# Square sums of q and k as rows with a 16-column table, their scales through DRAM, and values one unit sooner

## Chip, cores and metric

The kernel runs on one core of a Trainium2 chip. The metric is the device time of one execution in microseconds (us), the median of several.

## The reference

One layer of a hybrid encoder in float32, for a sequence of 1024 tokens and a width of 2048. After an RMSNorm, one projection gives the columns of two head groups. The change concerns group A, eight attention heads of 128 dimensions:

```python
qa = _rope_partial(_rmsnorm(q_a.reshape(B, S, ATT_HEADS, ATT_HEAD_DIM), q_norm_w), cos, sin)
ka = _rope_partial(_rmsnorm(k_a.reshape(B, S, ATT_HEADS, ATT_HEAD_DIM), k_norm_w), cos, sin)
```

So each head needs, for q and for k, the sum of squares of every token over the 128 dimensions, and its root's reciprocal as a factor of that token; the first 32 dimensions are rotated. Banded softmax attention over three dilated windows follows, and a gate silu(z). Group B is a matrix-memory mLSTM of four heads, run in both directions. Both outputs go through one output projection and are added to x.

## The kernel before

**Layout and units.** Everything is held transposed: dimensions on the 128 partitions, tokens along the free axis. The program is written by hand as a sequence of units `u`, the same for every engine: each engine has a loop over `u` that does its share of the main products, and then calls the functions of the side work with `at = u - start`. Units 0 to 447 are the input projection in a Strassen-like form of 7 products for each of 64 groups; units 448 to 575 are the output projection. A unit on TensorE (`product`, L649 on, or `out_product`) is 12 main matmuls of 128x512 (w_hi and w_lo against t_hi and t_lo, L671 to L675; L699 to L701 in the output). ScalarE rounds the weight block (w_hi, L933) and VectorE makes the rest (w_lo, L1158) two units ahead; both evict products (`evict`), VectorE also makes the sums s_tmp (L1193 to L1214) in most units. At the start of a unit VectorE evicts the unit before, so a late VectorE holds TensorE up once it is about one unit behind. There are two banks of PSUM for the products.

**The attention heads.** Head h starts at unit 357 + 18 h (`A_START`) and runs to at = 23, so that at 18 to 23 of one head are at 0 to 5 of the next. By `at`:
- SyncE (`attention_loads`) fetches raw q and k at -4, the 32 rows to be rotated at 2 (eight small transfers, L501), writes the rotated rows back over the raw ones at 5 and 6 (L508), fetches z at 6 (L514) and v at 8 (L518), and stores y at 23 (L521). SyncE issues all loads and most stores of the kernel in program order, the weights among them; a wait in it holds back what follows. POOL issues the accumulating stores of the products.
- ScalarE squares raw q and k into a_q and a_k at 0. TensorE sums them at 1 (`square_sums`, L824): 16 fp32 matmuls, each with 128 tokens of the squares as the stationary operand and one column of ones as the moving one. The tokens are taken with a step of 4 (`to_class`), so the result is one column of sums for each block of 128 tokens, on 128 partitions.
- VectorE adds eps at 2 (L1554), ScalarE takes the root (L1089), VectorE the reciprocal at 3 (L1561): 128x16 each. TensorE spreads the columns over all partitions at 3 and 5 (`spread`, 8 transposes of a repeated column each, into PSUM banks 4 to 7).
- VectorE rotates at 4 and 5 (`rotate`, in a_q and a_k), and makes the normed q and k at 7 and 9 (`normed`, L1514) from raw, weight and the spread scale in PSUM; z is scaled at 8 (L1548) and v at 10 (L1551).
- Then, for eight blocks of queries i: scores at 10 + i (L864 to L868), masked minimum on VectorE and exponentials on ScalarE at 11 + i, the division (VectorE L1537, ScalarE L1069) and TensorE's probability transposes (L881 to L884) at 12 + i, and their copies to pT by ScalarE (L1076) and VectorE (L1586) at 13 + i. pT holds two blocks. `values` (L895 to L899) of blocks 2j and 2j + 1 come at 15 + 2j, ahead of the probability transposes of the same unit; VectorE multiplies them by the gate at 16 + 2j (L1569). The copy of block 2j + 2 waits for values(j), and the probability transposes of a block wait for both copies of the block before:

```python
if i % 2 == 0 and i > 0:
    act.wait_ge(a_pv, 4 * g + i // 2)
```

**The gate stage.** In unit 42 the same kind of sums is taken of x for the first norm: 8 matmuls with contiguous tokens (L724) for xrsc and 8 with the step of 4 (L726) for eps in the order of the classes. In unit 45 eight transposes spread xrsc.

Of the kernel before, what the change touches and what calls it, by code (L numbers as in the profile page):

```python
# [108 lines left out]
def build_program(nc, xT, w_all, w_gates, vecs, norm_cols, m_cols, att_mask, rope, eye, tri, fin, part, y_dram, outT):  # L109
    with ExitStack() as ctx:  # L110
# [31 lines left out]
        xq = sb("xq", [P, 2 * TB])  # L142
# [5 lines left out]
        qk_arg = sb("qk_arg", [P, 2 * TB])  # L148
        qk_rms = sb("qk_rms", [P, 2 * TB])
        qk_rs = sb("qk_rs", [P, 2 * TB])  # L150
# [45 lines left out]
        pT = view(5504, 6 * 256).rearrange("p (b q) -> p b q", b=6)  # L196
        cos4, sin4 = view(11776, 256), view(12032, 256)
# [111 lines left out]
        a_bc = sem("a_bc")  # L309
# [66 lines left out]
        def _(sp):  # L376
# [100 lines left out]
            def attention_loads(h, at):  # L477
# [18 lines left out]
                if at == 2:  # L496
                    sp.wait_ge(a_ss, h + 1)
                    for i, to in enumerate((a_q, a_k)):
                        src = fin[2 * GROUPS[g[i]][0] + 1 - i]
                        for k in range(4):  # L500
                            sp.dma_start(to[k * ROT:(k + 1) * ROT, 0:256],  # L501
                                         src[k // 2, 0:ROT, k % 2 * 256:(k % 2 + 1) * 256]).then_inc(turn_in[i], 16)
                if at in (5, 6):
                    i = at - 5
                    raw, to = ((raw_a, a_q), (raw_b, a_k))[i]
# [13 lines left out]
                if at == 23:  # L519
# [124 lines left out]
        def _(pe):  # L644
# [62 lines left out]
            def gates_and_norm(u):  # L707
# [12 lines left out]
                if u == 42:  # L720
                    pe.wait_ge(xg_sum, KT)
                    pe.wait_ge(prep, 3)
                    for b in range(TB):
                        nc.tensor.matmul(ps[:, 5, b:b + 1], sq_acc[:, b * P:(b + 1) * P], ones[:, 0:1],  # L724
                                         start=True, stop=True)
                        mm = nc.tensor.matmul(ps[:, 5, TB + b:TB + b + 1],  # L726
                                              to_class(sq_acc)[:, b // 2, b % 2 * P:(b % 2 + 1) * P], ones[:, 0:1],
                                              start=True, stop=True)
                    mm.then_inc(x_ss, 1)
                if u == 45:  # L730
                    pe.wait_ge(x_rs, 1)
                    pe.wait_ge(consts, 64)
                    for b in range(TB):
                        t = on_all_partitions(flat(6)[:, b * P:(b + 1) * P], xrsc[:, b:b + 1])
                    t.then_inc(x_bc, 1)
# [79 lines left out]
            def square_sums(h):  # L815
                pe.wait_ge(a_sq, 2 * h + 2)
                if h > 0:
# [4 lines left out]
                for i, src in enumerate((a_q, a_k)):  # L822
                    for b in range(TB):
                        mm = nc.tensor.matmul(ps[:, 4, i * TB + b:i * TB + b + 1],  # L824
                                              to_class(src)[:, b // 2, b % 2 * P:(b % 2 + 1) * P],
# [985 lines left out]
```

## Time and profile before

| | |
|---|---|
| median of 3 runs | 2150.01 us (2148.2 to 2152.46) |
| the profiled execution's own time | 2148.27 us |
| its span, from the first to the last instruction | 2146.1 us |
| TensorE, matmuls | busy 2068.2 us (96%) |
| VectorE | busy 1292.6 us (60%) |
| ScalarE | busy 846.7 us (39%) |
| mean granted clock of TensorE | 0.977 of full |

Times in the profile are in microseconds unless marked ns. PE is TensorE's matmul, PEld its weight load (which overlaps PE), DVE VectorE, ACT ScalarE, POOL GpSimd, SP SyncE; a q behind a name is the engine's queue. L12 is line 12 of the kernel before. An fp32 matmul has two records in the trace, a transpose and a main matmul (fp32r) one. Records of TensorE are pipelined, so from start to start is the time that one costs, and the duration shown is longer. PEclk is the granted clock of TensorE as a share of 2.4 GHz.

### The profile page before, as it was taken

How to read it: one execution, taken by the hardware profiler on the slowest of the kernel's cores; microseconds unless marked ns; L12 is line 12 of the kernel's file. 1: busy time of each engine (PE TensorE's matmuls, PEld its weight loads, DVE VectorE, ACT ScalarE, POOL GpSimd, SP SyncE). 2: the span in 40 equal slices, each digit the busy share in tenths (PEclk: the TensorE clock that was granted, in tenths of full speed). 3: DMA queues.
4: the chain of work that ended last, by engine and by line, in shares of the span. 5: the costliest groups of instructions: out<-in, count | busy, mean ns of one | idle time of the engine just before them, and what ended most of it. 6: DMA issues, size and time to landing. Idle time of an engine off the chain costs nothing.

```text
span 2146.1 us, 27457 instructions
## 1 busy us (share of the span) xinstructions
PE 2068.2 (96%) x9536; PEld 1699.7 (79%) x9536; DVE 1292.6 (60%) x2670; ACT 846.7 (39%) x1350; POOL 174.0 (8%) x156
## 2 busy tenths in 40 slices
PE   5999999999999999999999999999998999999999
PEld 3887887888888888888878878778786877878887
DVE  7777758677677667767686646464565434343222
ACT  5553325344344335335453344352536343342110
POOL 4340000110110110010001101000010000000000
PEclk9999999999999999999999999999999999999999
DMA  4552344652562553463436535253344514235443
GB/s 161 181 162 79 113 139 141 142 133 79 142 148 84 132 130 108 119 146 99 137 133 163 112 67 130 57 115 84 89 99 142 192 53 149 77 113 183 147 140 111
DMA packets 140104, 264.62 MB, mean 123 GB/s; under 512 B 16320, under 2 KB 20928, under 8 KB 139712
## 3 DMA queue, kind: packets, MB, share of 16 engines
q1 hardware_dynamic: 121536, 229.32, 32.5%
q0 software_dynamic: 18432, 33.56, 11.1%
q8 instruction: 77, 1.26, 0.2%
q14 instruction: 59, 0.48, 0.1%
HBM read 168.44 MB, written 92.27 MB: 121 GB/s over the span
## 4 chain that ended last, share of the span: by engine, by line
PE 87%; DVE 4%; ACT 4%; issue 3%; DMA 1%; SPq 1%; DVEq 0%; ACTq 0%
PE ps L671 18%; PE ps L675 17%; PE ps L673 17%; PE ps L699 5%; PE ps L701 5%; PE ps L700 5%; PE ps L824 3%; PE ps L895 2%; PE ps L864 2%; PE ps L781 1%; PE ps L790 1%; PE ps L705 1%; PE ps L881 1%; PE ps L784 1%; PE ps L899 1%
## 5 line engine op out<-in xcount | busy, mean ns | idle before, releaser
L671 PE MATMUL ps<-t_hi,w_hi 128*128 128x512 f32 x1792 | 722.3, 403 | 40.4 <-DVE t_lo L1610 12.6
L675 PE MATMUL ps<-t_hi,w_lo 128*128 128x512 f32 x1792 | 705.6, 394 | 0.0
L673 PE MATMUL ps<-t_lo,w_hi 128*128 128x512 f32 x1792 | 705.5, 394 | 0.0
L671 PEld LDWEIGHTS ps<-t_hi,w_hi 128*128 128x128 f32 x1792 | 341.3, 190 | 115.6 <-issue 49.7
L675 PEld LDWEIGHTS ps<-t_hi,w_lo 128*128 128x128 f32 x1792 | 341.0, 190 | 73.9
L673 PEld LDWEIGHTS ps<-t_lo,w_hi 128*128 128x128 f32 x1792 | 342.0, 191 | 66.4
L933 ACT CAST w_hi<-w_raw 128x512 fp32r<-128x512 f32 x256 | 158.5, 619 | 427.7 <-PE ps L701 214.5
L1158 DVE TENSOR_TENSOR w_lo<-s_tmp,w_hi 128x512 fp32r<-128x512 f32 x256 | 182.2, 712 | 135.0 <-ACT w_hi L933 125.7
L933 ACT CAST w_hi<-s_tmp 128x512 fp32r<-128x512 f32 x256 | 158.6, 620 | 258.8 <-PE ps L675 239.2
L1158 DVE TENSOR_TENSOR w_lo<-w_raw,w_hi 128x512 fp32r<-128x512 f32 x256 | 182.1, 711 | 124.3 <-ACT w_hi L933 117.5
L699 PE MATMUL ps<-t_hi,w_hi 128*128 128x512 f32 x384 | 157.0, 409 | 0.7 <-DVE xt L1601 0.7
L701 PE MATMUL ps<-t_hi,w_lo 128*128 128x512 f32 x384 | 152.6, 397 | 0.0
L700 PE MATMUL ps<-t_lo,w_hi 128*128 128x512 f32 x384 | 152.5, 397 | 0.0
L1601 DVE TENSOR_TENSOR xt<-ps,s_tmp 128x512 f32<-128x512 f32 x64 | 44.0, 688 | 141.9 <-PE ps L701 141.9
L358 POOL DMA_DIRECT2D fin_dram<-xt x32 | 27.8, 870 | 952.1 <-ACT xt L946 952.1
L1586 DVE COPY arena<-ps 128x256 f32<-128x256 f32 x64 | 26.9, 420 | 110.7 <-PE ps L899 109.5
L699 PEld LDWEIGHTS ps<-t_hi,w_hi 128*128 128x128 f32 x384 | 74.2, 193 | 16.7 <-issue 2.5
L701 PEld LDWEIGHTS ps<-t_hi,w_lo 128*128 128x128 f32 x384 | 73.8, 192 | 16.3
L700 PEld LDWEIGHTS ps<-t_lo,w_hi 128*128 128x128 f32 x384 | 74.3, 193 | 14.4
L1076 ACT COPY arena<-ps 128x512 f32<-128x512 f32 x64 | 36.9, 577 | 115.1 <-PE ps L899 111.4
L1026 ACT ACTIVATE arena<-arena,g_cols 128x128 f32<-128x128 f32 x64 | 25.8, 403 | 130.8 <-DVE arena L1397 130.7
L941 ACT COPY xt<-ps 128x512 f32<-128x512 f32 x64 | 37.6, 587 | 95.4 <-PE ps L675 95.2
(216 smaller groups left out, 2858.0 us busy)
## 6 DMA issues: line engine op xcount, KB each, us to landing
w_raw<-w_all_dram SPq DMA_DIRECT2D x320, 256.0 KB, 3.5
fin_dram<-xt SPq DMA_DIRECT2D x128, 256.0 KB, 4.0
fin_dram<-xt POOLq DMA_DIRECT2D x128, 256.0 KB, 4.3
arena<-fin_dram SPq DMA_DIRECT2D x64, 512.0 KB, 5.1
arena<-xT_dram SPq DMA_DIRECT2D x48, 256.0 KB, 6.3
arena<-xT_dram SPq DMA_DIRECT2D x16, 512.0 KB, 3.8
y_raw<-y_dram SPq DMA_DIRECT2D x16, 512.0 KB, 5.0
s_tmp<-xT_dram SPq DMA_DIRECT2D x32, 256.0 KB, 4.0
```

What stands on the lines that cost most here:

```text
L671: nc.tensor.matmul(ps[:, bank, :], hi, t_hi[:, n, k, :], start=new and k == 0, stop=False, skip_group_check=True)
L673: nc.tensor.matmul(ps[:, bank, :], hi, t_lo[:, n, k, :], start=False, stop=False, skip_group_check=True)
L675: mm = nc.tensor.matmul(ps[:, bank, :], lo, t_hi[:, n, k, :], start=False, stop=k == KP - 1, skip_group_check=True)
L699: nc.tensor.matmul(ps[:, half, :], hi, yh, start=piece == 0 and k == 0, stop=False)
L700: nc.tensor.matmul(ps[:, half, :], hi, yl, start=False, stop=False)
L701: mm = nc.tensor.matmul(ps[:, half, :], lo, yh, start=False, stop=piece == 1 and k == KP - 1)
L824: mm = nc.tensor.matmul(ps[:, 4, i * TB + b:i * TB + b + 1], to_class(src)[:, b // 2, b % 2 * P:(b % 2 + 1) * P], ones[:, 0:1], start=True ...
L864: nc.tensor.matmul(ps[:, 4, :], q, by_class(a_k)[:, :, h * P:(h + 1) * P], start=True, stop=True)
L895: nc.tensor.matmul(out, vtok[:, 4 * h + b, :], pT[:, b, :], start=b == 0, stop=False)
L933: nc.scalar.copy(w_hi[:, b % 3, :], src).then_inc(hi_done, 1)
L1158: nc.vector.tensor_tensor(w_lo[:, b % 3, :], src, w_hi[:, b % 3, :].bitcast(F32), ALU.subtract).then_inc(lo_done, 1)
L1601: nc.vector.tensor_tensor(xt[:, e % 6, :], ps[:, e % 2, :], s_tmp[:, e % 3, :], ALU.add).then_inc(o_done, 1)
```

## The change

- **Square sums as rows.** A table `pick` of 31 columns, all zero but the middle one, is made once. In `square_sums` 16 columns of it are the stationary operand, and 128 contiguous tokens of the squares the moving one; the window into the table is shifted with each of the 16 matmuls, and all accumulate in 16x128 of PSUM bank 4, one row for each block of tokens. Argument, root and reciprocal are computed in place on 16 partitions x 128 (`qk_rs`, a view of a_cols); the argument is put into the order of the classes as it is read.
- **Scales through DRAM.** At 3 SyncE waits for the reciprocal and writes the 16 rows to `rs_dram` (two transfers in pieces of 128 bytes); at 5 it waits for them to land and reads the 1024 scales of q and of k onto all 128 partitions, into a_q and a_k (two transfers of 512 KB). `spread` is gone; `normed` reads the scale from SBUF.
- **The rotated rows** have buffers of their own (`turn`, in the place of prob), since a_q and a_k hold squares and then scales. SyncE loads them at 2 without waiting for the sums.
- **Values a unit sooner.** `values` run at 14, 16, 18 and 20, behind the probability transposes of the same unit; VectorE's product with the gate comes at 15, 17, 19 and 21, and y is stored at 22.
- **Gate stage.** The 8 stepped sums of x are gone. eps times the mean square is turned from columns into 16 rows by one transpose in unit 45 and copied to `eps_rows` in 46.

The diff, cut to its core:

```diff
@@ -139,15 +140,14 @@
         a_cols = sb("a_cols", [P, TB, 4, M_HEADS])
-        xq = sb("xq", [P, 2 * TB])
+        xq = sb("xq", [P, TB])
...
         epsx = sb("epsx", [P, 2, TB])
-        qk_arg = sb("qk_arg", [P, 2 * TB])
-        qk_rms = sb("qk_rms", [P, 2 * TB])
-        qk_rs = sb("qk_rs", [P, 2 * TB])
+        pick = sb("pick", [P, 4 * TB - 1])
+        eps_rows = sb("eps_rows", [P, P])
@@ -194,6 +194,8 @@
         pT = view(5504, 6 * 256).rearrange("p (b q) -> p b q", b=6)
+        turn = [view(4096, 512), view(4608, 512)]
+        qk_rs = a_cols.rearrange("p c k h -> p (c k h)")
@@ -306,7 +308,8 @@
         a_rs = sem("a_rs")
-        a_bc = sem("a_bc")
+        rs_out = sem("rs_out")
+        bc_in = sem("bc_in")
@@ -494,15 +497,28 @@
                 if at == 2:
-                    sp.wait_ge(a_ss, h + 1)
-                    for i, to in enumerate((a_q, a_k)):
+                    if h > 0:
+                        sp.wait_ge(a_t, 16 * h)
+                    for i, to in enumerate(turn):
...
                                          src[k // 2, 0:ROT, k % 2 * 256:(k % 2 + 1) * 256]).then_inc(turn_in[i], 16)
+                if at == 3:
+                    sp.wait_ge(a_rs, h + 1)
+                    for i in range(2):
+                        sp.dma_start(rs_dram[h, i].rearrange("r b n -> b r n"),
+                                     qk_rs[i * TB:(i + 1) * TB].rearrange("p (r n) -> p r n", r=CLASSES)
+                                     ).then_inc(rs_out, 16)
+                if at == 5:
+                    sp.wait_ge(rs_out, 32 * (h + 1))
+                    sp.wait_ge(a_ss, h + 1)
+                    for i, to in enumerate((a_q, a_k)):
+                        sp.dma_start(to, rs_dram[h, i].rearrange("r b n -> (r b n)").unsqueeze(0).to_broadcast([P, SEQ])
+                                     ).then_inc(bc_in, 16)
...
                     i = at - 5
-                    raw, to = ((raw_a, a_q), (raw_b, a_k))[i]
+                    raw, to = ((raw_a, turn[0]), (raw_b, turn[1]))[i]
@@ -516,7 +532,7 @@
                     sp.dma_start(halves(raw_a), fin_tile(g[0], 0)).then_inc(v_raw, 16)
-                if at == 23:
+                if at == 22:
@@ -721,10 +737,7 @@
                     for b in range(TB):
-                        nc.tensor.matmul(ps[:, 5, b:b + 1], sq_acc[:, b * P:(b + 1) * P], ones[:, 0:1],
-                                         start=True, stop=True)
-                        mm = nc.tensor.matmul(ps[:, 5, TB + b:TB + b + 1],
-                                              to_class(sq_acc)[:, b // 2, b % 2 * P:(b % 2 + 1) * P], ones[:, 0:1],
+                        mm = nc.tensor.matmul(ps[:, 5, b:b + 1], sq_acc[:, b * P:(b + 1) * P], ones[:, 0:1],
@@ -732,6 +745,8 @@
                         t = on_all_partitions(flat(6)[:, b * P:(b + 1) * P], xrsc[:, b:b + 1])
+                    pe.wait_ge(x_cols, 3)
+                    t = nc.tensor.transpose(ps[0:2 * TB, 5, 0:P], epsx.rearrange("p i b -> p (i b)"), ident[:])
@@ -814,25 +829,17 @@
                 pe.wait_ge(a_sq, 2 * h + 2)
+                pe.wait_ge(prep, 5)
...
                     pe.wait_ge(m_c, 16 * M_HEADS)
-                for i, src in enumerate((a_q, a_k)):
-                    for b in range(TB):
-                        mm = nc.tensor.matmul(ps[:, 4, i * TB + b:i * TB + b + 1],
-                                              to_class(src)[:, b // 2, b % 2 * P:(b % 2 + 1) * P],
-                                              ones[:, 0:1], start=True, stop=True)
+                for r in range(2 * TB):
+                    src = (a_q, a_k)[r // TB][:, r % TB * P:(r % TB + 1) * P]
+                    mm = nc.tensor.matmul(ps[0:2 * TB, 4, 0:P], pick[:, 2 * TB - 1 - r:4 * TB - 1 - r], src,
+                                          start=r == 0, stop=r == 2 * TB - 1)
                 mm.then_inc(a_ss, 1)
-
-            def spread(h, i):
-                pe.wait_ge(a_rs, h + 1)
-                if i == 1 and h > 0:
-                    pe.wait_ge(a_y, 4 * h)
-                for b in range(TB):
-                    t = on_all_partitions(flat(4 + 2 * i)[:, b * P:(b + 1) * P], qk_rs[:, i * TB + b:i * TB + b + 1])
-                t.then_inc(a_bc, 1)
@@ -902,16 +909,14 @@
                     square_sums(h)
-                if at in (3, 5):
-                    spread(h, (at - 3) // 2)
...
                     value_transposes(h)
-                if at in (15, 17, 19, 21):
-                    values(h, (at - 15) // 2)
...
                     prob_transposes(h, at - 12)
+                if at in (14, 16, 18, 20):
+                    values(h, (at - 14) // 2)
@@ -1086,7 +1091,7 @@
                     act.wait_ge(a_arg, h + 1)
-                    nc.scalar.activation(qk_rms[:], qk_arg[:], ACT.Sqrt).then_inc(a_rms, 1)
+                    nc.scalar.activation(qk_rs[0:2 * TB], qk_rs[0:2 * TB], ACT.Sqrt).then_inc(a_rms, 1)
@@ -1150,6 +1155,9 @@
             nc.vector.memset(spare[:, 1:2], 0.0).then_inc(prep, 1)
+            nc.vector.memset(pick[:], 0.0).then_inc(prep, 1)
+            dve.wait_ge(prep, 4)
+            nc.vector.memset(pick[:, 2 * TB - 1:2 * TB], 1.0).then_inc(prep, 1)
@@ -1297,12 +1305,12 @@
                     dve.wait_ge(x_ss, 1)
-                    nc.vector.tensor_scalar(xq[:], ps[:, 5, 0:2 * TB], 1.0 / D_MODEL, EPS, ALU.mult, ALU.add
+                    nc.vector.tensor_scalar(xq[:], ps[:, 5, 0:TB], 1.0 / D_MODEL, EPS, ALU.mult, ALU.add
...
                     for i in range(2):
-                        nc.vector.tensor_scalar(epsx[:, i, :], xq[:, TB:2 * TB], EPS, None, ALU.mult).then_inc(x_cols, 1)
+                        nc.vector.tensor_scalar(epsx[:, i, :], xq[:], EPS, None, ALU.mult).then_inc(x_cols, 1)
@@ -1312,6 +1320,7 @@
                     nc.vector.tensor_copy(xrs[:], flat(6)).then_inc(x_norm, 1)
+                    nc.vector.tensor_copy(eps_rows[0:2 * TB], ps[0:2 * TB, 5, 0:P]).then_inc(x_cols, 1)
@@ -1490,7 +1499,7 @@
-                to = a_q if i == 0 else a_k
+                to = turn[i]
@@ -1510,8 +1519,8 @@
                 dve.wait_ge(turned[i], 64 * (h + 1))
-                dve.wait_ge(a_bc, 2 * h + i + 1)
-                nc.vector.scalar_tensor_tensor(by_class(out), to_class(raw), w, by_class(flat(4 + 2 * i)),
+                dve.wait_ge(bc_in, 32 * (h + 1))
+                nc.vector.scalar_tensor_tensor(by_class(out), to_class(raw), w, by_class(out),
@@ -1551,16 +1560,17 @@
                     dve.wait_ge(a_ss, h + 1)
-                    nc.vector.scalar_tensor_tensor(qk_arg[:], ps[:, 4, 0:2 * TB], 1.0 / P,
-                                                   epsx.rearrange("p i b -> p (i b)"), ALU.mult, ALU.add
-                                                   ).then_inc(a_arg, 1)
+                    if h > 0:
+                        dve.wait_ge(rs_out, 32 * h)
+                    if h == 0:
+                        dve.wait_ge(x_cols, 6)
+                    nc.vector.scalar_tensor_tensor(by_class(qk_rs[0:2 * TB]), to_class(ps[0:2 * TB, 4, 0:P]), 1.0 / P,
+                                                   to_class(eps_rows[0:2 * TB]), ALU.mult, ALU.add).then_inc(a_arg, 1)
...
                     dve.wait_ge(a_rms, h + 1)
-                    if h > 0:
-                        dve.wait_ge(a_bc, 2 * h)
-                    nc.vector.reciprocal(qk_rs[:], qk_rms[:]).then_inc(a_rs, 1)
-                if at in (16, 18, 20, 22):
-                    j = (at - 16) // 2
+                    nc.vector.reciprocal(qk_rs[0:2 * TB], qk_rs[0:2 * TB]).then_inc(a_rs, 1)
+                if at in (15, 17, 19, 21):
+                    j = (at - 15) // 2
@@ -1804,7 +1814,8 @@
+    rs_dram = nc.dram_tensor("rs_dram", (ATT_HEADS, 2, CLASSES, TB, P // CLASSES), _mybir.dt.float32, kind="Internal").ap()
```

## Rows read from the trace of the kernel before

**Rows 1.** The page: its first line, and the shares of the chain that ended last.

```profile
span 2146.1 us, 27457 instructions
...
PE 87%; DVE 4%; ACT 4%; issue 3%; DMA 1%; SPq 1%; DVEq 0%; ACTq 0%
```

**Rows 2.** Timeline of TensorE, head 0's square sums: start, duration, engine, line, operation.

```profile
1187.30 0.39 PE L673 MATMUL ps<-t_lo,w_hi 128*128 128x512 f32 x1
1187.52 0.40 PE L675 MATMUL ps<-t_hi,w_lo 128*128 128x512 f32 x1
1187.76 7.40 PE L824 MATMUL ps<-ones,arena 128*128 128x1 f32 x32
1195.02 0.78 PE L671 MATMUL ps<-t_hi,w_hi 128*128 128x512 f32 x1
1195.59 0.63 PE L673 MATMUL ps<-t_lo,w_hi 128*128 128x512 f32 x1
1196.02 0.63 PE L675 MATMUL ps<-t_hi,w_lo 128*128 128x512 f32 x1
```

**Rows 3.** Windows: length, busy PE, PEld, DVE, ACT, POOL, then PEclk, DMA share, GB/s.

```profile
166.09:172.25 6.16, 6.16 (x34) 6.16 (x32) 2.51 (x4) 2.39 (x3) 0.00 (x0) 0.68 0.68 214
172.25:175.25 3.00, 3.00 (x8) 2.42 (x9) 0.17 (x1) 0.21 (x1) 0.00 (x0) 0.51 0.00 0
1195.00:1201.00 6.00, 6.00 (x19) 4.80 (x20) 0.80 (x2) 1.25 (x3) 0.15 (x1) 0.65 0.30 85
...
1855.70:1861.70 6.00, 6.00 (x16) 4.70 (x17) 1.03 (x3) 1.19 (x3) 0.00 (x0) 0.53 0.36 81
1180.00:1961.00 781.00, 746.65 (x3518) 606.83 (x3518) 389.03 (x985) 311.24 (x488) 46.69 (x54) 0.95 0.40 107
```

**Rows 4.** Waits of TensorE: us in total, times, longest.

```profile
PE ps L881 <- ACT arena L1076: 19.6, 24, 1.8
```

**Rows 5.** Timeline of VectorE and SyncE's queue, head 1, from reciprocal to z.

```profile
1290.51 0.24 DVE L1561 RECIPROCAL qk_rs<-qk_rms 128x16 f32<-128x16 f32 x1
...
1304.20 0.52 SPq L514 DMA_DIRECT2D arena<-fin_dram  x1
...
1306.16 2.03 DVE L1514 SCALAR_TENSOR_TENSOR arena<-arena,spare,ps 128x1024 f32<-128x1024 f32 x1
...
1309.90 1.22 DVE L1548 TENSOR_TENSOR arena<-arena,xrs 128x1024 f32<-128x1024 f32 x1
```

**Rows 6.** Timeline of TensorE, gate stage, sums with and without the step.

```profile
166.69 0.36 PE L724 MATMUL ps<-ones,arena 128*128 128x1 f32 x2
166.92 0.60 PE L726 MATMUL ps<-ones,arena 128*128 128x1 f32 x2
167.38 0.36 PE L724 MATMUL ps<-ones,arena 128*128 128x1 f32 x2
```

**Rows 7.** Timeline of TensorE, head 0, scores, values(0) and probability transposes.

```profile
1247.89 0.40 PE L868 MATMUL ps<-arena 128*128 128x128 f32 x2
1248.13 1.89 PE L895 MATMUL ps<-arena 128*128 128x256 f32 x8
...
1250.40 0.70 PE L899 MATMUL ps<-arena 64*128 64x256 f32 x2
1251.87 0.63 PE L881 MATMUL ps<-ident,arena 128*128 128x128 f32 x4 [0.78 <-ACT arena L1076]
```

**Rows 8.** The chain that ended last, head 0: start, us, what.

```profile
1202.67 0.87 PE ps L705 x8
```

**Rows 9.** Groups of VectorE by form: busy us, mean ns, idle before.

```profile
L1537 DVE RECIPROCAL sums<-sums 128x1 f32<-128x1 f32 x64 | 10.0, 157 | 9.2 <-ACT arena L1063 9.2
```

**Rows 10.** DMA issues: times, KB each, median us from issue to landing.

```profile
arena<-fin_dram SPq DMA_DIRECT2D x64, 512.0 KB, 5.1
...
arena<-arena SPq DMA_DIRECT2D x64, 32.0 KB, 1.9
...
arena<-rope_dram SPq DMA_DIRECT2D x1, 256.0 KB, 8.5
```

More of the change, by code:

```diff
@@ L106, in last_unit_of, with build_program @@
     return block if block < IN_UNITS else IN_UNITS + 2 * (block - IN_UNITS) + 1
-def build_program(nc, xT, w_all, w_gates, vecs, norm_cols, m_cols, att_mask, rope, eye, tri, fin, part, y_dram, outT):
+def build_program(nc, xT, w_all, w_gates, vecs, norm_cols, m_cols, att_mask, rope, eye, tri, fin, part, y_dram, rs_dram,
+                  outT):
     with ExitStack() as ctx:
@@ L1002, in gates_and_norm @@
                     act.wait_ge(x_cols, 1)
-                    nc.scalar.activation(xrms[:], xq[:, 0:TB], ACT.Sqrt).then_inc(x_rms, 1)
+                    nc.scalar.activation(xrms[:], xq[:], ACT.Sqrt).then_inc(x_rms, 1)
                 if u == 50:
@@ L1806 @@
     y_dram = nc.dram_tensor("y_dram", (KT, P, SEQ), _mybir.dt.float32, kind="Internal").ap()
+    rs_dram = nc.dram_tensor("rs_dram", (ATT_HEADS, 2, CLASSES, TB, P // CLASSES), _mybir.dt.float32, kind="Internal").ap()
     outT = nc.dram_tensor("outT_dram", (O_TILES, P, SEQ), _mybir.dt.float32, kind="ExternalOutput").ap()
-    build_program(nc, *args, fin, part, y_dram, outT)
+    build_program(nc, *args, fin, part, y_dram, rs_dram, outT)
     r = _run(nc, [arrays], core_ids=[0])
```

## The prediction

> **What bounds the kernel now.** I read the page first: of a span of 2146.1 us the chain that ended last runs 87% through TensorE [rows 1]. So the change is worth what it takes off TensorE, plus TensorE's waits that it ends, minus new ones. I then read TensorE's timeline around head 0's square sums [rows 2]. Main matmuls start every 0.22 to 0.23 us, then 32 records of square sums (two for each of 16 matmuls) hold the engine from 1187.76 to 1195.02, 7.3 us for 1/128 of the columns that they could stream, and afterwards main matmuls start every 0.43 us. The windows behind the sums show why: TensorE's granted clock is at 1.2 instead of 2.4 GHz for part of each [rows 3]. The list of waits of TensorE has one large entry in this stage, its probability transposes for ScalarE's copy at L1076, 24 times, 19.6 us [rows 4]. Last I read VectorE's and SyncE's timelines between the scales and the normed q of head 1 [rows 5], since the change lengthens that chain.
>
> **1. Square sums of a head.** Before, each record loads 128 columns of an operand with a step of 4 elements and streams one column: 7.3/32 = 0.23 us. The gate stage has both forms side by side: a pair of records with contiguous columns (L724) takes 166.92 - 166.69 = 0.23 us, a pair with the step (L726) 167.38 - 166.92 = 0.46 us, both at full clock [rows 6]. So it is the step in the stationary read that costs. After, the table has 16 adjacent columns and the 128 streamed columns are contiguous. The nearest row is an fp32 matmul of 128 streamed columns (L868), two records in 1248.13 - 1247.89 = 0.24 us [rows 7], 0.12 us each: 32 x 0.12 = 3.8 us. Saved: 8 x (7.3 - 3.8) = 28 us. Bounds: 0.23 us a record if a small table is no help (0 saved), 0.11 if it is a little (30 us). I take L868, the same streaming.
> The Trainium skill ("TensorE: Matmul & The Clock Gate", LDWEIGHTS) gives the load as columns divided by 1.2 GHz, whatever the layout: 107 ns for 128 columns. By that rule the old sums were 32 x 0.107 = 3.4 us already, and rebuilding them would gain nothing. The trace agrees for the contiguous pair and not for the stepped one, and the measurement decides.
>
> **2. The clock behind the sums.** In eight windows of 6 us after the sums, one a head, the mean clock is well below 1 (0.65 in the first, 0.53 in the last), and the eight shortfalls from 1 add up to 3.18 [rows 3]. At half clock that is 2 x 3.18 x 6 = 38 us, in which a main matmul takes 0.43 instead of 0.23 us [rows 2], so 47% is lost: 18 us. The falls came while the engine streamed single columns. With 128 columns in each record and only 3.8 us of it, I count all of it as regained. Bounds: 0 and 18. Inside the old sums the half clock cost nothing, since the records kept their pace of 0.23 us.
>
> **3. The spread.** Two groups of 8 transposes for each head leave TensorE, 0.87 us each on the chain [rows 8]: 16 x 0.87 = 14 us.
>
> **4. Values a unit sooner.** Before, in unit 15 (17, 19, 21) values(j) run and the next probability transposes follow them; those need the copy of the earlier ones, which may overwrite pT only when values(j) are done. So TensorE ends values at 1251.10, ScalarE copies, and the transposes start at 1251.87 after a wait of 0.78 us [rows 7]: three times a head [rows 4]. After, values close unit 14 (16, 18, 20), the copy of the next unit finds them done, and a whole product of 12 main matmuls (2.7 us) lies between. They read copies that the transposes just ahead of them in their unit have waited for, so no new wait. Saved 24 x 0.78 = 19 us; the rest of the 19.6 belongs to one longer wait in the stage where y is split, and stays. VectorE's product with the gate and the store of y move one unit forward too and free the buffers sooner; worth nothing.
>
> **5. Gate stage.** L724 and L726 together take 6.16 us; eight pairs of L724 remain, 1.8 us. 4.3 us saved, and of the 3 us behind them 98% were at half clock (mean 0.51) [rows 3], 1.4 us. The added transpose of 16 columns costs 0.1, one of eight in a group of 0.87 us [rows 8]. Net 5.6 us. The memsets of the table lie under the first loads: no cost, at most 0.2 us.
>
> **6. The new chain.** The argument, the root and the reciprocal now cover 128 elements on 16 partitions. A reciprocal of one element takes 0.157 us, of 16 0.24 us [rows 5, 9]: 6 ns an element, so 0.93 us for 128, and VectorE loses 0.7 us a head in a unit where it has waits. Then SyncE issues two writes (0.5 us each, the issue of the z row [rows 5]), waits for them, issues two broadcasts of 512 KB to 128 partitions (0.5 us each) and goes on to the turned rows. No row shows a write of 128-byte pieces or a broadcast. The nearest are a 32 KB transfer, 1.9 us to landing, and a 512 KB load, 5.1 us; the far end is 8.5 us, the rope table behind the mask [rows 10]. Sum from the start of the reciprocal: 0.9 + 1.0 + 1.9 + 1.0 + 5.1 = 9.9 us. Available before: 1306.16 - 1290.51 = 15.6 us in head 1 [rows 5]. From it go values(3) (3.0 us of TensorE, as values(0) from 1248.13 to 1251.10 [rows 7], moved a unit forward) and both spreads (1.7 us): 10.9 us. So the scales land just in time, with 1.0 us to spare.
> What is late next is what stands behind the broadcasts in SyncE's queue. The z row is issued at 1304.20 and used at 1309.90 [rows 5], with no slack; two more issues of 0.5 us make it 1.0 us later, and VectorE waits there with evictions and low parts behind it, for which TensorE waits a little later (it can be one unit behind, no more). I charge 8 x 1.0 = 8 us. Bounds: 0, and 20 us when the two broadcasts also slow the z and v loads by 1.5 us. SyncE's wait for the scales holds back weights and stores for about a unit, as its wait for the sums did; POOL's stores are not moved. No cost in either.
>
> **Sum.** 28 + 18 + 14 + 19 + 5.6 = 84 us off, 8 back: 76. The profiled execution took 2148.3 us, 1.7 below the median of 2150.0, so 2072 against its own time and 2074 as a median.
>
> **Rivals.**
> A. The clock falls all the same, because a table of 16 columns leaves 112 of 128 array columns idle. For it: in the trace the clock fell while little was streamed, and once ahead of the sums, after probability transposes and a wait. Against it: stretches of small matmuls with full tables kept it. Price: the 18 + 1.4 us stay, and half of the 32 records run at twice 0.12 us, 8 x 1.9 = 15 at most, 8 likely: 2074 + 27 = 2101.
> The Trainium skill (the same page, Part 3) says that with M below 128 most of the array sits idle; it says nothing of the clock there, and no row here shows a table of 16 columns.
> B. The round trip through DRAM is late, and the result is **slower than before**. Place: VectorE at unit 7 waits for both broadcasts, with evictions queued behind it; the v row, which starts only when q is normed, is late in turn. Price: 8 us for each us beyond the 10.9 available. It eats the 76 us from 10.9 + 9.5 = 20.4 us on. With both landings at the slow end of 8.5 us the trip is 19.9 us and the time 2074 + 8 x 9.0 = 2146; at 22 us it is 2163. For it: one load took 8.5 us, and accumulating stores share the engines. Against it: the median 512 KB load is 5.1 us.
> The Trainium skill ("DMA: Bandwidth & Descriptors", Specifications) says that pieces below 512 bytes are written by read-modify-write. The writes here are such pieces, but only 64 of them for a head; no run yet shows their landing.
> C. The sums do not get cheaper: a record keeps 0.23 us whatever the table. For it: nothing but that no row has a small table. The time is 2074 + 28 = 2102 with the clock regained.
>
> **How the numbers follow.** Forecast 0.67, A 0.17, B 0.10 (0.07 of it between 2090 and 2150, 0.03 slower than before), C 0.06. The forecast's own range is 2060 (nothing given back, sums at the low bound) to 2090 (20 us back); A and C end around 2101. The range 2056 to 2103 leaves out the late half of B and some of A, under 2 in 10. A measurement of this kernel tells 0.2%, 4.3 us, from no change. Faster by more than that 0.96, within it 0.01, slower 0.03.
>
> **What the profile after would show.** L824's successor with 256 records of about 0.12 us from start to start and 3.8 us a head; no transposes of qk_rs; main matmuls at 0.23 us right behind the sums and granted clock 1.00 there; no wait of 0.78 us behind values; ScalarE's list without it. A clock of 0.5 behind the sums is A, records of 0.23 us are C. VectorE waiting for a transfer from rs_dram ahead of its product at L1514 is B, and one ahead of the z row bears out the 8 us. I am wrong in the whole if TensorE's idle time in the attention stage grows past the 34 us that it has (781.0 less 746.65 us in the long window) [rows 3].

## The result and the profile after

The changed kernel took 2075.6 us (median of 4 runs, 2070.9 to 2077.9) beside 2151.2 us for the kernel before: ratio 0.9648, 95% interval 0.9627 to 0.9669. Forecast were 2074 us, in a range of 2056 to 2103.

The page of the kernel after, its first lines and the chain's shares, beside [rows 1]:

```profile
span 2072.3 us, 27209 instructions
...
PE 2004.4 (97%) x9393; PEld 1637.3 (79%) x9393; DVE 1302.0 (63%) x2673; ACT 849.7 (41%) x1350; POOL 173.8 (8%) x156
...
PE 86%; DVE 5%; issue 3%; ACT 2%; DMA 2%; SPq 1%; DVEq 0%; ACTq 0%
```

TensorE lost 64 us of busy time (2068.2 to 2004.4) and 10 us of idle time (77.9 to 67.9). Its timeline in head 0, which answers to [rows 2]:

```profile
1182.91 0.39 PE L691 MATMUL ps<-t_hi,w_lo 128*128 128x512 f32 x1
1183.23 3.67 PE L840 MATMUL ps<-arena,pick 128*16 128x128 f32 x32
1186.83 0.50 PE L687 MATMUL ps<-t_hi,w_hi 128*128 128x512 f32 x1
...
1187.40 0.39 PE L691 MATMUL ps<-t_hi,w_lo 128*128 128x512 f32 x1
1187.63 0.40 PE L687 MATMUL ps<-t_hi,w_hi 128*128 128x512 f32 x1
```

The sums take 1186.83 - 1183.23 = 3.6 us instead of 7.3, and the main matmuls behind them start every 0.23 us, not every 0.43. The windows, with the columns of [rows 3]: behind head 0's sums, the gate stage, the attention stage, and then two stretches in which the clock is newly low.

```profile
1186.80:1192.80 6.00, 6.00 (x27) 4.97 (x27) 2.68 (x5) 1.56 (x4) 0.86 (x1) 1.00 0.12 16
160.00:182.00 22.00, 22.00 (x111) 18.55 (x110) 16.27 (x30) 6.81 (x11) 0.12 (x1) 1.00 0.29 95
1180.00:1890.00 710.00, 686.20 (x3382) 547.61 (x3381) 396.86 (x982) 312.88 (x487) 44.88 (x52) 0.99 0.48 130
1547.00:1553.00 6.00, 3.39 (x8) 2.74 (x9) 6.00 (x8) 0.70 (x2) 0.00 (x0) 0.50 0.36 130
1721.00:1727.00 6.00, 6.00 (x14) 4.72 (x15) 4.77 (x4) 0.49 (x1) 0.00 (x0) 0.50 0.91 288
```

The gate stage in the kernel before, for comparison:

```profile
160.00:182.00 22.00, 22.00 (x97) 19.12 (x96) 11.65 (x22) 5.57 (x9) 0.00 (x0) 0.84 0.26 79
```

The clock holds behind the sums of all eight heads, and TensorE's idle time in the attention stage is 710.0 - 686.2 = 24 us, where it was 34. But at 1547 and 1721, around VectorE's product for q in heads 4 and 6, the clock is at 1.2 GHz; the kernel before had no fall at that place. The waits of TensorE say why (us in total, times, longest), to be held against [rows 4]:

```profile
PE ps L715 <- DVE xt L1611: 10.5, 5, 6.1
...
PE ps L687 <- DVE xt L1184: 7.8, 4, 6.3
...
PE ps L871 <- DVE mins L1540: 2.3, 3, 1.5
PE ps L888 <- ACT arena L1081: 1.8, 1, 1.8
```

The kernel before had, besides the row of [rows 4], these two for the same two lines (L881 is L888 now, L864 is L871):

```profile
PE ps L881 <- DVE arena L1586: 8.0, 6, 3.3
PE ps L864 <- DVE mins L1531: 5.0, 6, 1.8
```

The 24 waits for ScalarE's copy are one, and those for VectorE's half of the copies are gone. In their place TensorE waits for VectorE's evictions, 6.3 us once in head 4 and 6.1 us once in head 6. Behind VectorE stands a transfer, here in head 4 (SyncE's queue and VectorE; L510 writes the scales, L517 broadcasts them, L524 turns the rotated rows back, L1523 is the product that norms q, and L687 is TensorE):

```profile
1525.56 0.62 SPq L510 DMA_DIRECT2D rs_dram<-a_cols  x2
...
1530.87 1.30 SPq L382 DMA_DIRECT2D w_raw<-w_all_dram  x3
1532.28 0.84 SPq L517 DMA_DIRECT2D arena<-rs_dram  x2
1533.17 5.15 SPq L524 DMA_DIRECT2D arena<-arena  x8
...
1543.90 2.03 DVE L1523 SCALAR_TENSOR_TENSOR arena<-arena,spare 128x1024 f32<-128x1024 f32 x1 [7.24 <-DMA arena<-arena]
...
1549.61 0.77 PE L687 MATMUL ps<-t_hi,w_hi 128*128 128x512 f32 x1 [6.31 <-DVE xt L1184]
```

Three weight blocks of 256 KB and two broadcasts of 512 KB are issued within 2.3 us, the turned rows of q right behind them. The chain that ended last goes through one of these turned rows, 8.7 us in flight, where 1.9 was the median before [rows 10]:

```profile
1535.14 8.73 DMA arena<-arena
```

But the product waits for two things, the turned rows of q and both broadcasts, and the profile puts such a wait down to whichever landed last. So I read the broadcasts' own landing in head 4 too:

```profile
L517 SPq DMA_DIRECT2D arena<-rs_dram x2: 370/401/432, 1532.3 to 1532.7; - x2
DMA to landing us min/median/max: 7.3/8.7/10.1
```

The second broadcast took the 10.1 us and landed at 1532.7 + 10.1 = 1542.8, the turned rows landed at 1543.9, and VectorE had been free since 1543.9 - 7.2 = 1536.7. So the scales were 6.1 us late themselves, and the turned rows added only 1.1 us. Read in the same way, from the start of the reciprocal, in us:

| head | until both broadcasts landed | until VectorE was free for q's product |
|---|---|---|
| 0 to 3 | 8.1 to 9.2 | 11.0 to 12.5 |
| 4 | 18.2 | 12.1 |
| 5 | 11.6 | 6.8 |
| 6 | 15.7 | 9.2 |
| 7 | 11.7 | 6.8 |

The groups of VectorE (as [rows 9]) give the sum over the heads, and the price of the longer scale chain:

```profile
L1523 DVE SCALAR_TENSOR_TENSOR arena<-arena,spare 128x1024 f32<-128x1024 f32 x8 | 16.4, 2052 | 25.8 <-DMA arena<-arena 25.8
L1557 DVE TENSOR_TENSOR arena<-arena,xrs 128x1024 f32<-128x1024 f32 x8 | 9.8, 1221 | 8.5 <-DMA arena<-fin_dram 8.5
L1571 DVE RECIPROCAL a_cols<-a_cols 16x128 f32<-16x128 f32 x8 | 7.5, 933 | 0.0
```

The reciprocal costs the 0.93 us that were worked out. VectorE waits 25.8 us in heads 4 to 7 ahead of q's product, a wait that the kernel before did not have there; for 22.2 of them (6.1 + 4.7 + 6.6 + 4.8) the scales had not landed either. At the product of z (L1557) it waits less than before, where this row stood:

```profile
L1548 DVE TENSOR_TENSOR arena<-arena,xrs 128x1024 f32<-128x1024 f32 x8 | 9.8, 1224 | 14.7 <-DMA arena<-fin_dram 14.7
```

### The profile page after: what moved, and what is told of

The parts are those of the page before. It is cut to its first block, busy times and chain, and to the rows that moved or that the text cites. A ratio compares the mean times of both kernels' runs of the same rounds, so it can differ in the third digit from the quotient of the medians.

```text
span 2072.3 us, 27209 instructions
## 1 busy us (share of the span) xinstructions
PE 2004.4 (97%) x9393; PEld 1637.3 (79%) x9393; DVE 1302.0 (63%) x2673; ACT 849.7 (41%) x1350; POOL 173.8 (8%) x156
## 4 chain that ended last, share of the span: by engine, by line
PE 86%; DVE 5%; issue 3%; ACT 2%; DMA 2%; SPq 1%; DVEq 0%; ACTq 0%
PE ps L687 18%; PE ps L691 18%; PE ps L689 18%; PE ps L715 5%; PE ps L716 5%; PE ps L717 5%; PE ps L902 3%; PE ps L871 2%; PE ps L840 1%; PE ps L796 1%; PE ps L805 1%; PE ps L888 1%; PE ps L799 1%; PE ps L906 1%; SPq L524 1%
## 5 line engine op out<-in xcount | busy, mean ns | idle before, releaser
L687 PE MATMUL ps<-t_hi,w_hi 128*128 128x512 f32 x1792 | 718.4, 401 | 48.6 <-DVE t_lo L1620 12.6
L687 PEld LDWEIGHTS ps<-t_hi,w_hi 128*128 128x128 f32 x1792 | 338.9, 189 | 130.4 <-issue 64.3
L689 PEld LDWEIGHTS ps<-t_lo,w_hi 128*128 128x128 f32 x1792 | 339.7, 190 | 65.6
L1611 DVE TENSOR_TENSOR xt<-ps,s_tmp 128x512 f32<-128x512 f32 x64 | 43.9, 687 | 142.2 <-PE ps L717 142.1
L717 PEld LDWEIGHTS ps<-t_hi,w_lo 128*128 128x128 f32 x384 | 72.8, 190 | 15.7
L1031 ACT ACTIVATE arena<-arena,g_cols 128x128 f32<-128x128 f32 x64 | 25.8, 402 | 130.2 <-DVE arena L1406 130.2
L1190 DVE TENSOR_TENSOR xt<-ps,xt 128x512 f32<-128x512 f32 x64 | 44.1, 689 | 48.7 <-PE ps L691 48.3
L1074 ACT ACTIVATE arena<-arena,sums 128x704 f32<-128x704 f32 x64 | 56.4, 881 | 43.2 <-DVE sums L1546 43.2
```

The costliest lines, as they stand in the source:

```text
L687: nc.tensor.matmul(ps[:, bank, :], hi, t_hi[:, n, k, :], start=new and k == 0, stop=False, skip_group_check=True)
L689: nc.tensor.matmul(ps[:, bank, :], hi, t_lo[:, n, k, :], start=False, stop=False, skip_group_check=True)
L717: mm = nc.tensor.matmul(ps[:, half, :], lo, yh, start=False, stop=piece == 1 and k == KP - 1)
L1074: nc.scalar.activation(prob[:, i % 2, 0:KEYS], prob[:, i % 2, 0:KEYS], ACT.Copy, scale=sums[:, 2 + i % 2:3 + i % 2]).then_inc(a_p, 1)
L1190: nc.vector.tensor_tensor(x1, bank, x1, ALU.add).then_inc(ev_d, 1)
L1611: nc.vector.tensor_tensor(xt[:, e % 6, :], ps[:, e % 2, :], s_tmp[:, e % 3, :], ALU.add).then_inc(o_done, 1)
```

## The experiments

Each time is a median; the kernel before took 2148.9 to 2149.7 us beside them, and the changed kernel is taken at its 2075.6 (ratio 0.9648). The kernel before stood some 2 us higher beside that one (2151.2), so a difference of a run from the changed kernel is uncertain by 2 us beyond its interval.

**1. Values back at their old place.** The changed kernel with

```diff
-                if at in (14, 16, 18, 20):
-                    values(h, (at - 14) // 2)
```

after the probability transposes replaced by the lines of before, ahead of them (and the product with the gate and the store of y a unit later).

> The changed kernel (2076 us) with values back at 15, 17, 19, 21, ahead of the probability transposes. If TensorE's wait for the copy comes from that order, 24 waits of 0.78 us return before the probability transposes: 19 us, 2095 us. Rival: with the short sums the wait is hidden or was worth less, 2076 to 2080 us and fewer than 10 such waits.

2102.6 us, ratio 0.9785 (0.9771 to 0.9800): 27 us slower, not 19. The waits of TensorE:

```profile
PE ps L888 <- ACT arena L1081: 18.7, 24, 0.8
...
PE ps L888 <- DVE arena L1596: 7.9, 6, 3.2
...
PE ps L871 <- DVE mins L1540: 5.1, 6, 1.8
```

The 24 waits are back as forecast. With them come two that I had not counted: for VectorE's half of the same copies (7.9 us), and for the masked minimum (5.1 instead of 2.3). Both rows stood in the list of the kernel before.

**2. Values alone, in the kernel before.**

> The kernel before (2151 us) with values a unit sooner and nothing else. Order theory: the 24 waits of 0.78 us go, 2132 us. Rival: the time won is given back as waits of TensorE for VectorE or as a longer half clock, 2140 to 2151 us.

2112.0 us, ratio 0.9829 (0.9814 to 0.9843): 37 us, twice the forecast. The page's busy row, and what is left of the waits:

```profile
PE 2062.4 (98%) x9536; PEld 1699.5 (81%) x9536; DVE 1296.1 (61%) x2670; ACT 849.2 (40%) x1350; POOL 173.8 (8%) x156
```

```profile
PE ps L864 <- DVE mins L1531: 2.0, 3, 1.5
PE ps L881 <- ACT arena L1076: 1.8, 1, 1.8
```

Of its span of 2109.3 us 46.9 are idle on TensorE, 31 less than before: 18 from ScalarE's copy, 8 from VectorE's, 3 from the minimum. The other 6 us are busy time: the same matmuls, but with the clock low for less of it (mean over the span 0.980, against 0.977).

**3. No step in the old sums.** The kernel before with

```diff
-                                              to_class(src)[:, b // 2, b % 2 * P:(b % 2 + 1) * P],
+                                              src[:, b * P:(b + 1) * P],
```

in `square_sums`. The scales reach other tokens than they should.

> The kernel before with the stationary columns of q's and k's square sums taken contiguous instead of with a step of 4 (the scales then reach other tokens). Step theory: a record costs 0.115 us, 3.7 us a head instead of 7.3, at least 28 us less: 2122 us with the clock still falling behind the sums. If the fall depends on the length of the stretch with one column streamed and 3.7 us are too short for it, 18 us more go: 2104 us. Rival: the pace is set by the 128-column load itself, 0.23 us a record and 2151 us.

2127.6 us, ratio 0.9900 (0.9878 to 0.9923): 21 us. The group of the sums, 60.0 us busy before:

```profile
L824 PE MATMUL ps<-ones,arena 128*128 128x1 f32 x256 | 36.2, 276 | 0.0
```

24 us come off the sums by the step alone, 4.5 us a head instead of 7.5. The clock still falls in seven heads, during the sums or as they end (mean over the span 0.981, against 0.977 before and 0.992 after); in head 0, whose sums take 3.6 us, it holds. Head 2's sums take 4.06 us from 1363.47 on, and in a window that begins 3 us into them, with the columns of [rows 3], it is at 1.2 GHz throughout.

```profile
1363.47 4.06 PE L824 MATMUL ps<-ones,arena 128*128 128x1 f32 x32
```

```profile
1366.50:1373.30 6.80, 6.80 (x20) 5.54 (x20) 1.27 (x3) 0.56 (x2) 0.00 (x0) 0.50 0.33 89
```

So sums that stream single columns lose the clock in most heads even when they take little more than half the time. Where the clock falls early in them, as in head 4, they take 5.8 us and not 3.7; that keeps the gain below the 28 us forecast.

**4. An eighth of the broadcasts.** The changed kernel; scales of 128 of the 1024 tokens are broadcast, the others left out:

```diff
-                        sp.dma_start(to, rs_dram[h, i].rearrange("r b n -> (r b n)").unsqueeze(0).to_broadcast([P, SEQ])
+                        sp.dma_start(to[:, 0:P], rs_dram[h, i].rearrange("r b n -> (r b n)")[0:P].unsqueeze(0).to_broadcast([P, P])
```

> The changed kernel with the two broadcasts cut to the first 128 of 1024 scales (the others are left out), 64 KB each instead of 512. Traffic theory: the turned rows no longer queue behind 1 MB, VectorE's 25.8 us of waiting ahead of its normed q goes, and with it the waits of TensorE of 6.3, 6.1, 2.1 and 2.0 us in heads 4 to 7 and two falls of the clock: about 2057 us. Rival: it is SyncE's issue order and its wait for the scales that make the turned rows late, 2070 to 2076 us and the waits stay.

2063.4 us, ratio 0.9599 (0.9585 to 0.9613): 12 us faster.

```profile
PE ps L715 <- DVE xt L1611: 3.9, 5, 1.7
PE ps L687 <- DVE xt L1184: 3.4, 4, 1.9
```

The two waits of 6 us and the falls behind them are gone (mean clock 0.996); 7 us of the smaller waits stay. VectorE's wait ahead of q's product falls from 25.8 to 7.7 us, and the one for z grows from 8.5 to 19.1 us: in the trace both the broadcasts (median 3.7 us to landing, 6.1 in the changed kernel) and the turned rows (2.5, against 4.3) come sooner. So seven eighths of the 1 MB a head cost 12 us, not the 19 expected. Since both came sooner, this run does not tell late scales from late turned rows.

**5. Turned rows ahead of the broadcasts.** The same bytes in another order: turned rows of q, broadcast of q, turned rows of k, broadcast of k, z.

```diff
                                      ).then_inc(turned[i], 16)
+                    if i == 0:
+                        sp.wait_ge(rs_out, 32 * (h + 1))
+                        sp.wait_ge(a_ss, h + 1)
+                    sp.dma_start((a_q, a_k)[i], rs_dram[h, i].rearrange("r b n -> (r b n)").unsqueeze(0
+                                 ).to_broadcast([P, SEQ])).then_inc(bc_in[i], 16)
```

> The changed kernel with each head's turned rows of q issued ahead of the broadcast of q, and those of k ahead of the broadcast of k, each with its own semaphore, so that normed q waits for 512 KB less. Same bytes. Traffic theory: the turned rows land in 2 to 3 us, most of the 25.8 us wait ahead of normed q goes, 2060 us. Rival: the queues are full in that stretch whatever the order, the broadcast is then the late one, 2070 to 2078 us.

2090.3 us, ratio 0.9724 (0.9708 to 0.9741): 15 us slower than the changed kernel. VectorE's waits for transfers:

```profile
DVE arena L1556 <- DMA arena<-fin_dram: 25.6, 8, 4.6
DVE arena L1522 <- DMA arena<-rs_dram: 22.4, 8, 4.0
```

The turned rows are no longer waited for; in all eight heads the scales are, and z, which now stands behind a broadcast. The broadcasts had been leaving before the rotation was done, in time that was free; behind it they are late everywhere. My theory that the order alone would cure it fell, as the landing times of the broadcasts would have told: they were nearly as late as the turned rows.

**6. The new sums twice.** The second pass overwrites the first.

```diff
+                for again in range(2):
```

> The changed kernel with every head's square sums made twice (the second pass overwrites the first): 7.0 us of the 16-column table in a row, as long as the old sums. If streamed columns keep the clock whatever the table's width: 8 x 3.5 = 28 us more, 2104 us, and granted clock 1.00 in and behind the sums. If a 16-column table does not keep the clock and only the shortness of the stretch saved it: falls behind most heads as before, 2104 + 18 and more, 2122 us or above, with clock 0.5 in the windows.

2105.3 us, ratio 0.9791 (0.9777 to 0.9805): 30 us more. Head 0 on TensorE, and the windows of the first heads with the columns of [rows 3]:

```profile
1182.09 7.16 PE L841 MATMUL ps<-arena,pick 128*16 128x128 f32 x64
```

```profile
1182.00:1192.00 10.00, 10.00 (x77) 8.49 (x77) 2.35 (x4) 0.93 (x2) 0.00 (x0) 1.00 0.11 28
...
1180.00:1561.00 381.00, 374.30 (x1937) 300.62 (x1936) 224.49 (x545) 168.59 (x269) 38.94 (x45) 1.00 0.49 112
```

7.2 us of narrow-table matmuls in a row, as long as the old sums, and the clock stays at 2.4 GHz over four heads. In heads 4 to 7 it holds through and behind the doubled sums too, which take 7.2 us each; the four falls there come 23 us or more behind them, in waits of TensorE for VectorE's evictions of 2.3 to 7.6 us. Rival A's cause is out: a table of 16 columns with 128 streamed ones kept the clock, where one of 128 columns with a single streamed one lost it in seven heads of eight (run 3).

**7. A full table.** The identity, 128 columns, in place of the 16-column window; the sums over the dimensions are left out.

```diff
-                    mm = nc.tensor.matmul(ps[0:2 * TB, 4, 0:P], pick[:, 2 * TB - 1 - r:4 * TB - 1 - r], src,
+                    mm = nc.tensor.matmul(ps[:, 4, 0:P], ident[:], src,
```

> The changed kernel with the 128x128 identity as stationary operand of the square sums in place of the 16-column table (the sums over the dimensions are left out; same number of matmuls and streamed columns). If the narrow table brings nothing by itself and the pace is that of the 128 streamed columns: 0.11 to 0.12 us a record, 2076 us. Rival: the narrow load is what makes it quick, 0.19 to 0.23 us a record, 8 x 32 x 0.08 = 20 us or more on top, 2096 us.

2073.5 us, ratio 0.9642 (0.9627 to 0.9657), no difference that can be told.

```profile
L840 PE MATMUL ps<-arena,ident 128*128 128x128 f32 x256 | 29.9, 275 | 0.0
L840 PEld LDWEIGHTS ps<-arena,ident 128*128 128x128 f32 x256 | 29.3, 192 | 0.1
```

The load is twice as long (192 ns, against a median of 97 with 16 columns) and the sums take the same time (29.3 us with the narrow table): in the trace it overlaps the 128 streamed columns and costs nothing.

**8. The step on the streamed side.** The changed kernel, with the 128 streamed columns taken with the step of 4; the rows then hold the sums in another order.

```diff
-                    src = (a_q, a_k)[r // TB][:, r % TB * P:(r % TB + 1) * P]
+                    src = to_class((a_q, a_k)[r // TB])[:, r % TB // 2, r % TB % 2 * P:(r % TB % 2 + 1) * P]
```

> The changed kernel with the 128 streamed columns of each square sum taken with the step of 4 (rows then hold the sums in another order). If the step costs the same on the streamed side as on the stationary side: 0.23 us a record, 28 us more, 2104 us. If only the stationary load suffers: 0.11 us, 2076 us.

2104.4 us, ratio 0.9787 (0.9774 to 0.9801): 29 us slower.

```profile
L840 PE MATMUL ps<-arena,pick 128*16 128x128 f32 x256 | 59.4, 405 | 0.0
```

7.4 us a head again, as the old sums had. The step costs the same on either side.

**9. Broadcasts at 4.** The changed kernel with `if at == 5` ahead of the wait for rs_out made `if at == 4`.

> The changed kernel with both broadcasts issued at 4 instead of 5, nothing else. In head 4 SyncE stood 4.3 us at the weights of the next group (unit 5 is the first of a group there) between writing the scales (1525.56) and broadcasting them (1532.28); in the heads without that wait the gap is 1.6 us. Queue-order theory: in head 4 the broadcasts leave 5 us sooner, its 6.3 us wait of TensorE and the fall behind it go, as in head 6: 12 to 16 us less, 2062 us. Rival (traffic alone): the engines are as full whenever the 1 MB comes, 2072 to 2078 us.

2069.6 us, ratio 0.9626 (0.9611 to 0.9641), 6 us below the changed kernel with overlapping intervals. SyncE's queue in head 4:

```profile
1525.07 0.62 SPq L510 DMA_DIRECT2D rs_dram<-a_cols  x2
...
1526.77 0.84 SPq L517 DMA_DIRECT2D arena<-rs_dram  x2
1530.39 1.66 SPq L382 DMA_DIRECT2D w_raw<-w_all_dram  x3
1532.09 4.99 SPq L524 DMA_DIRECT2D arena<-arena  x8
```

The broadcasts leave 5.5 us sooner, ahead of the weights. In this profile TensorE's longest wait there is 2.4 us and the fall of the clock in head 4 is gone. So in head 4 the place behind the wait for the weights made the long wait; the theory holds there: the scales land 1.3 us before VectorE is free, and only the turned rows are late, by 3.4 us. But the expected 12 to 16 us in total did not come: in heads 5 to 7 VectorE still waits 4.7 to 5.4 us, and the scales still land 2.5 to 4.5 us after it is free.

**10. The two broadcasts apart.** As 9, with that of k at 5, behind the turned rows of q.

> The changed kernel with the broadcast of q's scales at 4, and that of k's at 5 behind the turned rows of q, each with its own semaphore. Half the bytes are then ahead of the turned rows of q. If bytes ahead of the turned rows are the cost, better than both broadcasts at 4: 2058 us. If their place in the queue was all, the same as that one within 3 us; if k's broadcast now delays z as with the turned rows first (2090 us), 2070 us or more.

2069.0 us, ratio 0.9628 (0.9615 to 0.9642): the same as 9. VectorE waits less for the turned rows (11.5 us, 18.9 in 9) and more for z (21.5 us, 10.2 in 9). The wait moves, the time does not.

**11. The old spreads twice.** The kernel before, each group of 8 transposes made twice.

> The kernel before (2149 us) with each spread's 8 transposes made twice. If the spreads lie on TensorE's path with their whole length, 16 x 0.87 = 14 us more: 2163 us. Rival: they lie in units where TensorE waits for VectorE later anyway, under 5 us more, 2150 to 2154 us; or transposes make the clock fall more, 2170 us and above.

2159.0 us, ratio 1.0046 (1.0032 to 1.0060): 10 us for a doubling priced at 14. TensorE's busy time grew by 10.8 us.

**12. z ahead of k's turned rows, on top of 9.**

```diff
+                if at == 6:
+                    if h > 0:
+                        sp.wait_ge(a_out, 16 * h)
+                    tile_done(sp, g[1], 1)
+                    sp.dma_start(halves(ystage), fin_tile(g[1], 1)).then_inc(z_raw, 16)
                 if at in (5, 6):
...
-                if at == 6:
...
```

> The kernel with both broadcasts at 4, and z issued at 6 ahead of the turned rows of k instead of behind them. There VectorE waits 10.2 us in five heads for z (needed in unit 8) while the turned rows of k are needed in unit 9 only. If z's place behind four small transfers is what remains of the give-back: those waits go and 3 to 6 us come off, 2064 to 2067 us. Rival: 512 KB of z then delay the turned rows of k, or those of q that share the engines, 2070 us or more.

2061.5 us, ratio 0.9590 (0.9576 to 0.9604). This is the version that beats both kernels: its interval lies wholly below the changed kernel's. VectorE's waits for transfers:

```profile
DVE arena L1523 <- DMA arena<-arena: 17.6, 4, 5.1
DVE arena L1557 <- DMA arena<-fin_dram: 6.3, 3, 3.1
```

The wait for z falls from 10.2 to 6.3 us, and the turned rows are not later. That is less than the 8 us that the median gained, so how all of it came is open. The traces cannot tell: the profiled execution of this run was its slowest (2065.2 us) and that of run 9 one of its fastest (2064.7 us).

## Why the prediction was right

That the total came out within 2 us was luck: two terms were wrong by some 10 us each and cancelled. In the traces, the waits that values removed are 17.8 + 8.0 + 2.7 = 28.5 us of TensorE's idle time and not 19, and the waits that came in are 67.9 - (77.9 - 28.5) = 18.5 us and not 8. TensorE's busy time fell by 64 us, where steps 1, 2, 3 and 5 gave 66; but 6 of the 64 came with values (2010.8 in run 1 to 2004.4), from which I had counted none.

- **Step 1, the sums: right.** 3.6 us a head against 3.8 forecast; doubling them cost 30 us (run 6), and the step explains the old 7.3 (runs 3 and 8, both ways). The rule of the Trainium skill ("TensorE: Matmul & The Clock Gate", LDWEIGHTS), columns divided by 1.2 GHz with no term for the step between them, would have made this gain nothing. The trace disagrees with it for a step of 4 elements: 0.23 us a record. That the table is narrow, as the change has it, brought nothing (run 7); the contiguous columns did.
- **Step 2, the clock: right in kind.** No fall at the sums of any head, and run 6 shows that the clock would hold in a stretch twice as long. But I counted no new falls, and two came in the waits of 6 us in heads 4 and 6. Some 9.4 us of matmuls ran at half clock in them; by the 47% of step 2 that is 4 us, an estimate.
- **Step 3, the spreads: right in kind, too large if anything.** They lie on TensorE's path; the doubling showed 10 us for the 14. Removing them was not run by itself.
- **Step 4, values: mis-sized.** I took 19 us from the one row of the wait list with the large number; one wait of 1.8 us in that row stays, so the row itself gave 17.8. Alone the move gave 37 us (run 2), in the company of the rest 27 (run 1). Of the 10 us between them, 5.6 are TensorE's waits for evictions (L1611, L1184), which are that much longer with values sooner than in run 1. The term left out VectorE's half of the same copies, 8.0 us, that stood in the same list, the 3 us of waits for the masked minimum, and 6 us of clock. The mechanism was the one argued.
- **Step 5, the gate stage: right in kind.** The stepped sums are gone, the clock over 160 to 182 us is 1.00 where it was 0.84, and head 0's sums start 4.5 us sooner, against 5.6 forecast; other differences of the two executions ahead of it are in that number.
- **Step 6, the give-back: the path was wrong, and the size.** The reciprocal was as worked out, 0.93 us, and in heads 0 to 3 the scales took 8.1 to 9.2 us against 9.9 forecast and came in time. In heads 4 to 7 they came 4.7 to 6.6 us late, for three reasons that the sum did not have. I read the 10.9 us available in head 1 alone: they were 6.8 in heads 5 and 7. I took 5.1 us for a landing: the later broadcast took 8.5 to 10.1 there. And SyncE came to the broadcasts of heads 4 and 6 only 4.4 to 6.7 us after it began to write the scales, behind other issues and, in head 4, 4.3 us of waiting ahead of a weight load. The turned rows of q, small transfers issued behind the 1 MB, landed 0.8 to 1.1 us later still. I named z as the next to be late; it is waited for less than before. In run 1, where the values' gain is taken out, the change is worth 2148.9 - 2102.6 = 46 us, where steps 1, 2, 3, 5 and 6 gave 28 + 18 + 14 + 5.6 - 8 = 58. The two traces put 8 of the missing 12 us into TensorE's busy time, which fell by 57.4 us (2068.2 to 2010.8) instead of 65.6, and 4 into its idle time, which grew by 11.7 instead of 8. Spreads worth 10 and not 14 (run 11) would be half of the first, and matmuls at half clock in that run's four new falls may be the rest; no run splits them.
- **The bounds.** 2060 and 2090 do not follow from the terms beside them, which give 2074 - 8 - 2 = 2064 and 2074 + 12 = 2086.
- **Rivals.** A is refuted as a cause by run 6, and C by the 0.11 us a record. B came true in half of the heads: its place was right, VectorE at unit 7 with evictions queued behind, and so was its cause, scales that land after VectorE is free. The sign that I gave for it, a wait for a transfer from rs_dram, did not show, because the turned rows landed a little later and the wait is put down to them. Its price was too high: 8 us for each us of lateness would be 22 us for the 22.2 us over the eight heads, and nearly all bytes taken away gave 12 back (run 4). How much the late scales cost without the late turned rows was not run. The rule on pieces below 512 bytes ("DMA: Bandwidth & Descriptors", Specifications, of the Trainium skill) showed no cost that mattered here: SyncE waits for the landing of both writes of 128-byte pieces, and the broadcasts left 1.6 us after the start of these writes in head 1 as in head 3.

## What to carry to other kernels

Before a matmul is priced by its shape, look at the step of both its operands. When a wait between two engines is taken away, add up every row of the wait list that ends in the same instruction, and not only the largest. When a change puts a longer chain ahead of a wait, read the time that it has in every head, not in one: here it was 12.5 us in one and 6.8 in another. When an instruction waits for several transfers, read the landing of each, since the wait list names only the last. And when a change adds bytes to a shared queue, ask which small transfer is issued right behind them; here the time and order of issue were worth 14 us (run 12).

## What the runs showed of the hardware that I had not expected

- A step of 4 fp32 elements doubles the time of a 128-column operand, on the streamed side as on the stationary one: 59.4 us against 29.3 for the same 256 records (run 8).
- 7.2 us of matmuls with 16 stationary and 128 streamed columns keep the granted clock at 2.4 GHz (run 6); during sums that stream one column it fell even when they took only 4.06 us (run 3, head 2), and held in head 0 of that run, where they took 3.6 us.
- A 32 KB transfer took 8.7 us to land when SyncE had issued 1.75 MB in the 4.3 us before it, against a median of 1.9 before. The second of the two 512 KB broadcasts ahead of it took 10.1 us, against 5.3 in head 1.
